# Loading the modulation weights two steps behind the weights they share a queue with, and splitting a third chunk before the normalised rows

## The reference

```python
h = rmsnorm(x, attn_pre_norm); proj = h @ w_in            # first block
...                                                       # three kinds of attention
x = x + rmsnorm(mixed @ w_out, attn_post_norm)
h = rmsnorm(x, ffn_pre_norm)
u = causal_depthwise_conv(h @ w_up, conv_w, conv_b)       # 3 taps along the tokens
gate, up = split(u)
x = x + rmsnorm((gelu(gate) * up) @ w_down, ffn_post_norm)

for layer in range(2):                                    # second block
    shift_m, scale_m, gate_m, shift_f, scale_f, gate_f = split(silu(c) @ ada_w[layer] + ada_b[layer], 6)
    h = rms_norm(x, g0) * (1 + scale_m) + shift_m
    x = x + gate_m * mixer(h)                             # attention in layer 0, retention in layer 1
    h = rms_norm(x, g1) * (1 + scale_f) + shift_f
    x = x + gate_f * swiglu(h)
return rms_norm(x, final_norm)
```

## Time and profile before

| | us |
|---|---|
| runs, median of three | 1119.11 (1114.18, 1119.11, 1119.61) |
| the profiled execution | 1112.1 |
| its span, first to last instruction | 1110.3 |
| busy: PE, DVE, ACT, POOL | 1047.6, 809.1, 588.4, 156.6 |
| mean granted TensorE clock | 0.988 of full |
| moved by DMA | 226.66 MB, mean 204 GB/s |

### The profile page before, as it was taken

One profiled execution on the slowest core, in us unless ns is written; L12 is line 12 of the kernel. 1 busy time (PEld: TensorE's weight loads), 2 busy tenths in 40 slices (PEclk: granted clock), 3 DMA queues, 4 the chain that ended last, 5 costly groups with the idle time before them and its releaser, 6 DMA issues.

```text
span 1110.3 us, 20499 instructions
## 1 busy us (share of the span) xinstructions
PE 1047.6 (94%) x7901; PEld 991.6 (89%) x7901; DVE 809.1 (73%) x1392; ACT 588.4 (53%) x1014; POOL 156.6 (14%) x162
## 2 busy tenths in 40 slices
PE   6988978899898989999999999999999999999998
PEld 5877778899776879799999999997899999999997
DVE  5767578899977788768899888877457657544443
ACT  5576367566523557657544444634365556444442
POOL 0000015333400120003211101200010013111010
PEclk9999998999999989999999999999999999999999
DMA  9630252856588543334799878464434554554450
GB/s 360 226 117 37 86 212 114 335 233 240 216 312 321 226 145 133 115 146 181 304 364 367 349 280 333 179 224 158 147 122 150 189 184 153 190 189 153 158 181 38
DMA packets 33536, 226.66 MB, mean 204 GB/s; under 512 B 3731, under 2 KB 4028, under 8 KB 9788
## 3 DMA queue, kind: packets, MB, share of 16 engines
q1 hardware_dynamic: 33020, 223.10, 54.0%
q0 software_dynamic: 448, 2.63, 0.7%
HBM read 224.66 MB, written 2.63 MB: 205 GB/s over the span
## 4 chain that ended last, share of the span: by engine, by line
PE 69%; DVE 14%; ACT 6%; DMA 6%; issue 2%; POOL 2%; SPq 0%; DVEq 0%; ACTq 0%; POOLq 0%
PE psum L1345 18%; PE psum L1347 18%; PE psum L1346 18%; DVE w_lo L2052 5%; DMA raw<-in_down 4%; ACT w_hi L746 3%; DVE arena L2156 2%; PE psum L1410 2%; PE psum L1413 2%; PE psum L1412 2%; POOL arena L699 1%; DMA raw<-in_up 1%; DVE arena L2307 1%; DVE arena L2346 1%; DVE hid_lo L2137 1%
## 5 line engine op out<-in xcount | busy, mean ns | idle before, releaser
L2052 DVE TENSOR_TENSOR w_lo<-raw,w_hi 128x1024 fp32r<-128x1024 f32 (+1 forms) x342 | 398.0, 1187 | 196.4 <-ACT w_hi L746 189.5
L746 ACT ACTIVATE w_hi<-raw 128x1024 fp32r<-128x1024 f32 (+1 forms) x342 | 334.3, 997 | 258.6 <-PE psum L1347 173.4
L1345 PE MATMUL psum<-h_hi,w_hi 128*128 128x256 f32 (+1 forms) x1144 | 328.0, 287 | 14.6 <-DVE arena L2346 8.6
L1346 PE MATMUL psum<-h_lo,w_hi 128*128 128x256 f32 (+1 forms) x1144 | 322.8, 282 | 0.0
L1347 PE MATMUL psum<-h_hi,w_lo 128*128 128x256 f32 (+1 forms) x1144 | 321.6, 281 | 0.0
L1345 PE MATMUL psum<-hid_hi,w_hi 128*128 128x256 f32 (+1 forms) x952 | 273.2, 287 | 15.9 <-DVE w_lo L2052 12.5
L1347 PE MATMUL psum<-hid_hi,w_lo 128*128 128x256 f32 (+1 forms) x952 | 270.4, 284 | 0.0
L1346 PE MATMUL psum<-hid_lo,w_hi 128*128 128x256 f32 (+1 forms) x952 | 270.4, 284 | 0.0
L1345 PEld LDWEIGHTS psum<-h_hi,w_hi 128*128 128x128 f32 x1144 | 216.2, 189 | 18.6 <-DVE arena L2346 9.3
L1346 PEld LDWEIGHTS psum<-h_lo,w_hi 128*128 128x128 f32 x1144 | 217.1, 190 | 0.7 <-issue 0.7
L1347 PEld LDWEIGHTS psum<-h_hi,w_lo 128*128 128x128 f32 x1144 | 217.1, 190 | 0.0
(11 more groups left out here) (265 smaller groups left out, 1179.1 us busy)
## 6 DMA issues: line engine op xcount, KB each, us to landing
arena<-in_ada SPq DMA_DIRECT2D x48, 1024.0 KB, 4.8
raw<-in_gu SPq DMA_DIRECT2D x44, 1024.0 KB, 4.8
raw<-in_ret_in SPq DMA_DIRECT2D x24, 1024.0 KB, 4.7
raw<-in_up SPq DMA_DIRECT2D x22, 1024.0 KB, 6.8
raw<-in_dn SPq DMA_DIRECT2D x32, 704.0 KB, 5.5
raw<-in_qkv SPq DMA_DIRECT2D x12, 1024.0 KB, 5.5
raw<-in_down SPq DMA_DIRECT2D x11, 1024.0 KB, 6.9
raw<-in_ret_o SPq DMA_DIRECT2D x8, 1024.0 KB, 4.8
```

The source lines that it names most:

```text
L746: nc.scalar.activation(w_hi[chunk % SPLIT_SLOTS][:, a:b], raw[chunk % RAW_SLOTS][:, a:b], ACT.Copy)\
L1345: nc.tensor.matmul(out, w[0], hc, start=start, stop=False, skip_group_check=True)
L1346: nc.tensor.matmul(out, w[0], lc, start=False, stop=False, skip_group_check=True)
L2052: tt(w_lo[s][:, a:b], raw[chunk % RAW_SLOTS][:, a:b], w_hi[s][:, a:b].bitcast(F32), ALU.subtract)\
```

## The change

1. The load of a piece now comes two steps behind the weights of its step (`ADA_LATE`) in `up`, `down`, `dn0` and `gu1` as well.
2. Pieces are dealt out anew: `up` 11 to 9, `down` 10 to 9, `gu0` 17 to 16, `gu1` 0 to 4 (steps 10 to 13). For the last, the vector `c` is loaded again and passed through silu again on ACT, since its place in the arena has been overwritten.
3. A table of 832 KB for the attention of layer 0 (`tab2`) was loaded ahead of all weights of `up`, behind a wait for the last tiles of the attention's output; it is now loaded at step 5 of `up`, and the wait with it.
4. Behind a row phase, the third chunk is split before the tiles of `h` (ACT: one half before the root, one behind it; DVE: right behind the root's refinement), the fourth between the tiles. The first two chunks are copied out earlier, and PE spreads 1/rms after 8 blocks of the second chunk, not 11.
5. `by_rows` goes bank by bank in the first chunk of a phase, too (both halves of the contraction for one bank, then the next).
6. In `up`, DVE splits chunk 4 before the taps of chunk 1, not after them.
7. Loops: DVE's in `gu0` now begins at step 4, not 10; DVE's steps in `gu1` are all written out; ACT's in `gu1` begins at 10; SP's leads are longer.

```diff
-ADA_STEPS = [("w_in", 10, lambda c: int(c in (KA, QA0))), ("up", 22, lambda c: int(c >= 5 and c % 2 or c in (6, 20))),
-             ("down", 11, lambda c: int(c < 10)), ("gu0", 22, lambda c: int(4 <= c <= 20)), ("dn0", 16, lambda c: c % 2)]
+ADA_STEPS = [("w_in", 10, lambda c: int(c in (KA, QA0))), ("up", 22, lambda c: int(5 <= c <= 20 and (c % 2 or c == 20))),
+             ("down", 11, lambda c: int(c < 9)), ("gu0", 22, lambda c: int(4 <= c <= 19)), ("dn0", 16, lambda c: c % 2),
+             ("gu1", 22, lambda c: int(10 <= c <= 13))]
+
+ADA_LATE = 2
...
-                    late = 2 if ph.name == "gu0" else 0
+                    if ph.name == "up" and step.i is None and step.j == 5:
+                        sp.wait_ge(h_tiles, tiles_before(FFNPRE))
+                        sp.dma_start(arena[:, TAB2_AT:TAB2_AT + dram["tab2"].shape[1]], dram["tab2"]).then_inc(tab2_in, 16)
+                    if ph.name == "gu1" and step.j == 9:
+                        sp.wait_ge(h_tiles, tiles_before(FINAL))
+                        sp.wait_ge(ada_out, ada_before("gu1", 0))
+                        sp.dma_start(cond_silu, dram["cond"]).then_inc(cond_in, 16)
+                    late = 0 if ph.name == "w_in" else ADA_LATE
...
-                steps(sp, ph.n, *{"up": (8, 0), "gu0": (12, 1)}.get(ph.name, (4, 0)), one)
-                for c in (20, 21) if ph.name == "gu0" else ():
+                steps(sp, ph.n, *{"up": (10, 0), "gu0": (12, 1), "dn0": (6, 0), "gu1": (18, 0)}.get(ph.name, (4, 0)), one)
+                for c in (ph.n - 2, ph.n - 1) if ph.name != "w_in" else ():
...
-                if ph.name == "up":
-
-                    sp.wait_ge(h_tiles, tiles_before(FFNPRE))
-                    sp.dma_start(arena[:, TAB2_AT:TAB2_AT + dram["tab2"].shape[1]], dram["tab2"]).then_inc(tab2_in, 16)
...
             def start_deferred(i):
                 ph = PH[AHEAD[i]]
+                if i in ROW_STAGE:
+                    hi(ph.chunk0 + 2, ahead=0)
                 root(i)
+                if i in ROW_STAGE:
+                    hi(ph.chunk0 + 2, ahead=1)
+                    leave_first(ph, i, 0)
...
                     round_tile(i, k)
+                    if i in ROW_STAGE and k == 2:
+                        leave_first(ph, i, 1)
                     if k in (3, 4):
-                        hi(ph.chunk0 + 2, ahead=k - 3)
-                leave_first(ph, i, 0)
-                leave_first(ph, i, 1)
-                hi(ph.chunk0 + 3)
+                        hi(ph.chunk0 + (3 if i in ROW_STAGE else 2), ahead=k - 3)
...
+                    if ph.name == "gu1" and step.j == 9:
+                        act.wait_ge(cond_in, 32)
+                        nc.scalar.activation(cond_silu, cond_silu, ACT.Silu).then_inc(cond_ready, 1)
...
-                steps(act, ph.n, 4, 1, step_)
+                steps(act, ph.n, 10 if ph.name == "gu1" else 4, 1, step_)
...
-                if last:
+                if last or c == 0:
                     order = [(k, r, n) for r in range(2) for n in range(2) for k in range(2)]
...
-            swiglu_phase("up", FFNPRE, 1, 11)
+            swiglu_phase("up", FFNPRE, 1, 8)
...
-            deferred_phase("qkv", L0, 1, spread_at=11)
+            deferred_phase("qkv", L0, 1, spread_at=8)
...
                 rstd(i)
+                if i in ROW_STAGE:
+                    lo(ph.chunk0 + 2)
...
                     if k in (4, 6):
-                        lo(ph.chunk0 + 2, ahead=(k - 4) // 2)
-                lo(ph.chunk0 + 3)
+                        lo(ph.chunk0 + (3 if i in ROW_STAGE else 2), ahead=(k - 4) // 2)
...
             taps_settled(0)
+            lo(ph.chunk0 + 4)
             taps_settled(1)
-            lo(ph.chunk0 + 4)
             taps_settled(2)
...
+                    if ph.name == "gu1" and c == 10:
+                        dve.wait_ge(cond_ready, 2)
...
-                steps(dve, ph.n, 10 if ph.name == "gu0" else 4, 1, one)
+                steps(dve, ph.n, 14 if ph.name == "gu1" else 4, 2, one)
```

More of the change, by code:

```diff
@@ L970, in start_deferred @@
                     round_tile(i, k)
+                    if i in ROW_STAGE and k == 2:
+                        leave_first(ph, i, 1)
                     if k in (3, 4):
-                        hi(ph.chunk0 + 2, ahead=k - 3)
-                leave_first(ph, i, 0)
-                leave_first(ph, i, 1)
-                hi(ph.chunk0 + 3)
+                        hi(ph.chunk0 + (3 if i in ROW_STAGE else 2), ahead=k - 3)
+                if i not in ROW_STAGE:
+                    leave_first(ph, i, 0)
+                    leave_first(ph, i, 1)
+                    hi(ph.chunk0 + 3)
             hi(PH["up"].chunk0)
@@ L2323, in norm_deferred @@
                     if k in (4, 6):
-                        lo(ph.chunk0 + 2, ahead=(k - 4) // 2)
-                lo(ph.chunk0 + 3)
+                        lo(ph.chunk0 + (3 if i in ROW_STAGE else 2), ahead=(k - 4) // 2)
+                if i not in ROW_STAGE:
+                    lo(ph.chunk0 + 3)
             row_copies(PH["w_out"], FFNPRE)
```

## The result

The changed kernel takes 1086.0 us (median; 1083.05 to 1088.71) where the kernel before takes 1116.64 beside it (1113.88 to 1119.61): a ratio of 0.973, 95% interval 0.968 to 0.977. Forecast were 1090 (1081 to 1105) and a gain of 27.9 us of the span. The span went from 1110.3 to 1083.7, by 26.6. The profile before comes from an execution of 1112.1 us, 4.5 under the median beside it, the one after from an execution of 1085.5, 0.5 under.

A forecast was written before the change was run, and what follows sets the result against it. PE was taken as the bound, busy 1047.6 of 1110.3 us. Terms 14.1 + 3.1 + 2.2 + 4.7 + 5.9 - 2.1 = 27.9 us off 1112.1 gave 1084.2; the median was set at 1090, range 1081 to 1105.

The forecast's parts named there:

- the 0.4 of part 3: Turned rows at the end of `down`: start some 2.6 us behind PE's last row, a gain of 0.4 us.
- the ring: In `down`, SP's piece waits for DVE to reduce the piece two before, holding the weights behind it: some 6.7 us a step.
- the 6.7 of a step: In `down`: the ring makes a step take some 6.7 us where PE needs 5.57.
- the piece of step 6 in SP's list: In `up`: a piece waiting for the first to be reduced held weights, causing gaps at chunks nine and ten; gain 3.1 us.
- the 2.6 of the forecast: Turned rows after `w_out` and `down`: with splits out of the way both start some 2.6 us behind PE's last row.
- the sum of DVE's and ACT's steps: Fourth chunk of `up`: `h` and a split on DVE to 169.2, ACT's copies to 170.0; before, the third ended about 175.
- leave a gap of about 3 and its dip in place: Sixth chunk of `up`: a gap of about 3 us and the low clock behind it stay; part 4 gains 4.7 there.
- in `gu0` DVE is the pace: `gu0`: DVE sets the pace, 5.62 us a written-out step, 5.82 looped, 6.11 over a trip's end; loss 2.1.
- A (DMA bound): Rival: two loads a step hold `down` near 6.2 us a step; it gives 8, not 14: 1096 us, chance 0.13.
- B (given back): Rival: third chunk's gain goes into new waits at the sixth of `up` and fourth of `qkv`: 1102 us, chance 0.13.
- C: Rival, slower: late pieces hold DVE and everything behind it; at 1.3 us a load 1130 us, chance 0.03.
- D: Rival: nothing comes of it, PE's waits are hidden behind a rate that stays the same: 1116 us, chance 0.03.

The follow-up runs named there:

- part 1 alone: The kernel before with pieces loaded two steps late in `up`, `down` and `dn0`, all else old: 1108.54 us, 0.992 of the kernel before.
- the run with the old order: The changed kernel with the first chunk of `w_out` and `down` in the old order (half the contraction for all four banks, then the second): 1094.6 us, one run.
- both kernels that fill the gap: Changed kernel, `gu0` written out, 12 filling matmuls behind third chunks of `up` and `qkv`: 1085.48 us; filling only `qkv`, DVE's and ACT's `up` written out too: 1081.3.

## Why the prediction was right, and where its terms were off

**Part 1 in `down`, 14.1 forecast, 13.7 measured** (75.75 to 62.05, from the first matmul to the last; the other 0.5 of the 14.25 lies behind it and belongs to the 0.4 of part 3). The mechanism held: the ring, not the bytes, set the steps (the kernel with loads not late shows it), and DMA delivered what 5.57 us a step asks, with more to spare than I had thought (407 GB/s, not 385). What I had not seen is how the sum divides. In the kernel before, the first chunk of `down` took 14.1 us and the sixth to tenth 6.5 to 6.7, while the second to fourth took 5.6: the stall at the start let the loads run ahead, so stall and ring hid part of each other. Over the whole stretch part 1 alone takes away 7.0; everything but the late loads in `down` 3.8; both 14.25. At the start two other parts are needed: without the new dealing a gap of 3.0 is left, without part 5 one of 2.1. I had the price of the whole from PE's count of matmuls (75.75 less 61.3). That is why the term came out right, although I gave to part 1 what takes parts 2 and 5 as well, and although the 6.7 of a step held for half of the steps only.

**Part 1 in `up`, 3.1 forecast, 3.9 measured**, the upper bound: the stretch lost both gaps wholly. My reason, the piece of step 6 in SP's list, was right in its place but not in its cause alone: the old dealing puts 3.0 of it back with the loads still late, and part 1 alone gained 1.8 of `up`. The two extra pieces of `up` fill the same queue.

**Part 2 in `gu1`, 0.** Not settled by the sum: the stretch is 2.6 longer, but not by the four steps (last section). Taking the pieces out of `up` and `down` was worth 7.6 us, which the prediction counted under part 1.

**Part 3, 1.8 and 0.4.** 1.85 measured, and 2.07 when the table goes back. From the point where PE is free of its last row to the turned rows it is 2.57 us in both places, the 2.6 of the forecast, where it was 4.45 and 3.09. But the 0.5 at the end of `down` is not the table's: it is there with part 1 alone, and it stays when the table goes back.

**Part 4 in `up`, 4.7 forecast, 6.1 measured.** The fourth chunk starts 4.65 earlier relative to the turned rows (29.92 to 25.27), as the sum of DVE's and ACT's steps said. The step that failed is "leave a gap of about 3 and its dip in place" at the sixth chunk. The sixth follows the fourth by 14.1 us in any case; but now the low clock came in the fourth chunk, where that row of steps hides it, and not in the sixth (5.76 us for 48 matmuls, 7.24 before). That is the other 1.5, and it is not part 4's own: the sixth chunk kept the full clock with part 4 undone (5.76), and lost it with part 4 in place in the run with the old order (7.29). Of the 4.65, undoing part 4 takes 4.0 back, so part 4 is worth 4.0, the other parts 0.7, and 1.5 is luck with the clock. Part 6 was not undone by itself.

**Part 4 in `qkv`, 5.9 forecast, 3.5 measured: a term mis-sized.** The fourth chunk starts 5.48 earlier. But PE reaches it 1.54 us before its data, and I gave that gap no price in clock. 48 matmuls of the fourth chunk take 7.65 us where the granted clock falls and 6.12 where it doesn't, 5.74 before. Nine profiles have this gap, of 1.5 us; in four the clock fell (27.6 for the stretch), in five not (26.1). So the term is 3.5 or 5.1 by chance; both kernels that fill the gap had 5.0 to 5.1.

**Part 7, -2.1 forecast and measured,** and given back by the written-out loop to 0.01 us. The size is in part luck. At 0.19 a looped step and 0.29 a trip's end the sixteen looped steps of the changed kernel should give back 4.2 us when all are written out, and the eight of the kernel before should have cost 2.1 already. They cost nothing: `gu0` took 116.54 with them and takes 116.53 with none, and PE's chunks take 5.76 us in both from the sixth on. The step that was wrong is "in `gu0` DVE is the pace". PE is, at 5.76 a chunk, and DVE at 5.62 a written-out step has 0.14 to spare. A loop costs only what it takes beyond PE's pace, 0.17 a step in the changed kernel ((3 x 5.82 + 6.26) / 4 less 5.76), some 2.7 us for sixteen steps less what DVE had gained before; for the eight steps before it was 0.13 (with 6.11 at the trip's end), 1.0 in all, and the six steps written out ahead of them could cover most of that. These last figures are an estimate from the rows; measured are 2.1 for the loop of sixteen steps and nothing for that of eight. The Trainium skill names a stalled fetch behind a taken branch (Runtime: NRT & Kernel Launch, "Instruction fetch mechanics"). The trace shows two prices, one of them at no branch: 0.19 us for each step in the loop, and 0.44 more where a trip ends. The page speaks only of the second, and that the 0.44 is such a stall is not shown.

**The rivals.** A (DMA bound) is out: steps at 5.57, 374 GB/s, and 407 where the buffers were being filled. B (given back) is right in one point, the new wait at the fourth chunks, which takes 0.4 us of `qkv`, or 1.9 where the clock falls, and nothing of `up`. C is out: no wait of DVE for a piece appears in `down`, and `down` takes what PE asks. D is out.

Against the runs' medians the gain is 30.6 us and against the spans 26.6; the start of the program alone varies by 4.7 us between profiles of one kernel, so the nearness of the total to the forecast is worth less than that of the terms.

## What to carry to other kernels

When one queue issues two streams, and one of them can wait for a consumer, issue that stream some steps behind the other; the price of not doing so is paid by the stream that could have gone. Price a stage by the count of its matmuls at full rate, not by adding up its gaps, and don't expect the parts of a change to add: here 7.0 and 3.8 alone made 14.25 together. Write a loop out where its engine would fall behind the one that sets the pace (2.1 and 2.3 us here; eight looped steps that stayed within PE's pace cost nothing), and where a gap is moved, ask what clock the work behind it will get and whether anything waits for that work.

## What the runs showed of the hardware

**Two paces at full clock.** The stretch from the start of `gu1` to the end of `dn1` takes 189.95 to 189.98 us or 192.55 to 192.57, and nothing between. These are windows of 60 us in `gu1` of four kernels, in order: before, after, the one with loads in `down` not late, and the old dealing with `gu0` written out.

```profile
1010.00:1070.00 60.00, 60.00 (x510) 60.00 (x509) 29.06 (x37) 26.55 (x41) 6.57 (x8) 1.00 0.48 157
```

```profile
1010.00:1070.00 60.00, 60.00 (x502) 60.00 (x501) 29.34 (x37) 27.54 (x40) 5.04 (x5) 1.00 0.41 132
```

```profile
1010.00:1070.00 60.00, 60.00 (x509) 60.00 (x508) 29.20 (x39) 26.05 (x39) 6.50 (x7) 1.00 0.47 157
```

```profile
1010.00:1070.00 60.00, 60.00 (x503) 60.00 (x502) 28.86 (x38) 25.65 (x38) 5.76 (x6) 1.00 0.45 150
```

PE is never idle and the clock is 1.00, yet a matmul starts every 118 ns or every 120. The third kernel has the same `gu1` with the same four pieces as the second and runs at the faster pace; the fourth has no piece in `gu1` and runs at the slower. So neither the pieces nor the code of `gu1` decide it. In all, the stretch took the shorter time in four profiles and the longer in ten. What picks the pace was not found; 2.6 us of this kernel hang on it.

**The same gap with and without the low clock.** At the start of `down` a gap of 3.04 us was followed by the lower clock in one profile and one of 3.03 was not in another; at the sixth chunk of `up` gaps of 2.46, 2.63, 2.64 and 2.98 were followed by it and one of 2.59 was not; the gaps of 1.5 in `qkv` went four and five ways. A gap's length alone does not say whether the clock falls.
